# Sample attention's bias rows, spread queries and long bias products, made inside compression

## What is computed

```python
def nsa_global(q, qpos, kv_cmp, kv_slc, p, rel_bias):
    blk, end_pos = compress_blocks(kv_cmp, p["cmp_w"], p["cmp_pe"])      # "compression"
    kc = rmsnorm(blk[:, :, 0], p["nsa_qk_norm"][1])
    o_cmp, p_cmp = cmp_attention(q, qpos, kc, blk[:, :, 1], end_pos, rel_bias)
    idx, valid = select_blocks(p_cmp, qpos, end_pos, n_slc)
    ...                                                                  # selected 64-token blocks
    bias = rel_g[rel_bucket(dist), gi[..., None]]                        # one bias per bucket and head
    pr = masked_softmax(s + bias, mask, axes=(-2, -1))

def sample_layer(...):
    o_cmp, o_slc = nsa_global(q, pos, full_c, full_s, p, rel_bias)
    o_win = win_attention(q[:, None], pos[None, :], win_kv[:, None], kpos, rel_bias)[:, 0]
    o_mem = mem_attention(qm, cache_mem)
    y = layer_tail(x, gb, o_pool, o_nsa, o_mem, p)                       # ends in the experts
```

## Time and profile before

| | |
|---|---|
| median of 3 runs | 1854.88 us (1852.64 to 1856.59) |
| the profiled execution, its own time | 1856.81 us |
| its span, first to last instruction | 1854.8 us |
| mean granted TensorE clock | 0.949 of full speed |
| PE busy | 1714.4 us (92%) |
| DVE, ACT, POOL busy | 550.5, 338.1, 449.9 us |
| compression | from 175 to 303 us |
| sample attention | from 304 to 382 us |

### The profile page before, as it was taken

How to read it: one execution, slowest core, us unless ns; L and a number is a source line. 1 busy time by engine, 2 the same in 40 slices (tenths; PEclk the granted TensorE clock), 3 DMA queues, 4 the chain that set the end, 5 groups by cost and what they waited for, 6 DMA issues and landing times.

```text
span 1854.8 us, 40016 instructions
## 1 busy us (share of the span) xinstructions
PE 1714.4 (92%) x16080; PEld 953.3 (51%) x16080; DVE 550.5 (30%) x1391; ACT 338.1 (18%) x740; POOL 449.9 (24%) x520
## 2 busy tenths in 40 slices
PE   7998997679799999879999999999999999999992
PEld 3446785244478884534465754444444444444441
DVE  1333113446401113453232313231323232323235
ACT  3232112146400001101111111111111111111110
POOL 1122326647400006011212212221212222222220
PEclk9997997779999999879999999999999999999996
DMA  9534757850251103339999999999999999999986
GB/s 342 198 104 150 252 162 221 278 210 2 84 165 57 52 25 119 139 151 404 425 422 425 416 421 411 428 423 421 422 421 408 427 423 420 423 420 406 430 338 248
DMA packets 86641, 541.98 MB, mean 292 GB/s; under 512 B 19888, under 2 KB 44048, under 8 KB 73617
## 3 DMA queue, kind: packets, MB, share of 16 engines
q1 hardware_dynamic: 64809, 498.50, 66.8%
q0 software_dynamic: 14544, 32.03, 5.1%
q10 hardware_dynamic: 7232, 10.73, 1.8%
HBM read 523.39 MB, written 29.78 MB: 298 GB/s over the span
## 4 chain that ended last, share of the span: by engine, by line
PE 54%; DMA 1%; DVE 0%; issue 0%; SPq 0%; POOLq 0%; POOL 0%; ACT 0%
PE psum L2987 36%; PE psum L3013 18%; DMA arena<-y_of 1%; PE psum L2997 0%; DVE arena L2977 0%; SPq L2826 0%; SPq L2828 0%; DMA y_of<-arena 0%; DMA arena<-scr_h,arena 0%; DVE arena L2920 0%; POOL arena L2857 0%; POOLq L2788 0%; ACT arena L2906 0%; POOLq L2861 0%; POOLq L2857 0%
## 5 line engine op out<-in xcount | busy, mean ns | idle before, releaser
L2987 PE MATMUL psum<-arena 128*32 128x512 f32 x6144 | 668.2, 592 | 2.7 <-issue 2.7
L2987 PEld LDWEIGHTS psum<-arena 128*32 128x32 f32 x6144 | 234.4, 108 | 417.0 <-issue 413.3
L3013 PE MATMUL psum<-arena 128*32 128x256 f32 x6144 | 344.9, 378 | 0.0
L3013 PEld LDWEIGHTS psum<-arena 128*32 128x32 f32 x6144 | 236.0, 109 | 110.0 <-issue 9.6
L2942 DVE TENSOR_TENSOR arena<-psum,arena 128x512 f32<-128x512 f32 x96 | 66.5, 692 | 582.4 <-PE psum L2987 582.4
L2874 POOL DMA_INDIRECT y_of<-arena x96 | 97.0, 1011 | 476.2 <-ACT arena L2906 476.2
L2902 ACT ACTIVATE arena<-arena 128x256 f32<-128x256 f32 x96 | 40.1, 418 | 610.1 <-DVE arena L2944 610.1
L2618 PE MATMUL psum<-arena 128*128 128x272 f32 x608 | 144.3, 395 | 1.6 <-PEq L235 1.6
L2618 PEld LDWEIGHTS psum<-arena 128*128 128x128 f32 x608 | 116.1, 191 | 28.5 <-issue 3.3
L2853 POOL DMA_INDIRECT arena<-scr_h,arena x96 | 98.8, 1030 | 48.9 <-POOL arena L2849 28.2
L878 PE MATMUL psum<-arena 128*128 128x512 f32 (+1 forms) x256 | 97.4, 541 | 12.7 <-DMA arena<-in_w_tok 10.1
(11 more groups left out here) (369 smaller groups left out, 1520.5 us busy)
## 6 DMA issues: line engine op xcount, KB each, us to landing
arena<-in_w_gu SPq DMA_DIRECT2D x64, 4096.0 KB, 15.1
arena<-in_w_down SPq DMA_DIRECT2D x32, 4096.0 KB, 14.5
arena<-in_w_gb SPq DMA_DIRECT2D x24, 512.0 KB, 4.5
arena<-y_of SPq DMA_DIRECT2D x8, 1024.0 KB, 15.3
arena<-in_cache_cmp SPq DMA_DIRECT2D x62, 128.0 KB, 3.1
arena<-in_cache_slc SPq DMA_DIRECT2D x60, 128.0 KB, 6.5
arena<-in_x_all SPq DMA_DIRECT2D x8, 512.0 KB, 11.3
arena<-in_w_tok SPq DMA_DIRECT2D x2, 2048.0 KB, 14.0
```

The costliest lines, as they stand in the source:

```text
L2987: mm = pe.matmul(gu_bank(g)[32 * j:32 * j + 32].rearrange("p (h n) -> p h n", h=2), xgT[:, g, 32 * k:32 * k + 32], gu_w(slot)[:, part, :, ...
L3013: mm = pe.matmul(dn_half(g)[32 * j:32 * j + 32], actT[:, g, 32 * k:32 * k + 32], dn_w(slot)[:, part, 256 * j:256 * j + 256], start=(k == 0 ...
```

## The change

The 14 DVE instructions that fill `rel_rows`, `q_rows` and `qm_rows`, with their three clears, move into compression, into a function `tables()` that DVE runs once, after `after(3)` and ahead of the copies of fill product 3. The four long bias products move to the end of PE's compression list: one ahead of `blocks(8)`, two ahead of `keys(8)`, one after it. Sample attention begins with the three short products; PE marks the four banks as full at once. ACT copies the banks in the order 2, 3, 0, 1. `q_rows` and `sc_m` swap places in SBUF, so that `q_rows` doesn't lie in memory that compression uses; the sizes of the two are the same.

```diff
                 for s in range(NS - 1):
                     after(s)
+                    if s == 3:
+                        tables()
                     if s < FILL:
...
+                pe.wait_ge(s_sc, 16 * 12)
+                pe.wait_ge(s_rr, 4)
+                def far_bias(*quarters):
+                    for q in quarters:
+                        pe.matmul(bank(q), rel_rows, oh_slc[:, 512 * q:512 * q + 512], start=True, stop=True).then_inc(s_b3, 1)
+                far_bias(2)
                 blocks(NS)
+                far_bias(3, 0)
                 keys(NS)
+                far_bias(1)
+                pe.wait_ge(s_qr, 12)
...
             def _(act):
-                for b in range(4):
+                for b in (2, 3, 0, 1):
                     filled(act, b, "bias", b)
+                    act.wait_ge(s_b3, 4)
                     copy(bias_slc[:, 512 * b:512 * b + 512], bank(b)).then_inc(free[b], 1)
...
             def _(dve):
-                dve.wait_ge(s_sc, 16 * 12)
-                link(dve.memset(rel_rows, 0.0))
-                for t in range(TS):
...
-                link(dve.memset(q_rows, 0.0))
-                link(dve.memset(qm_rows, 0.0))
...
             def _(pe):
-                pe.wait_ge(s_sc, 16 * 12)
-                pe.wait_ge(s_rr, 4)
+                for q in range(4):
+                    pe.sem_inc(full[q], 1)
                 pe.matmul(bank(5)[:, 0:NCMP_S], rel_rows, oh_cmp, start=True, stop=True).then_inc(full[5], 1)
                 pe.matmul(bank(6)[:, 0:32], rel_rows, oh_new, start=True, stop=True).then_inc(full[6], 1)
                 pe.matmul(bank(4), rel_rows, oh_win, start=True, stop=True).then_inc(full[4], 1)
-                for q in (2, 3, 0, 1):
-                    pe.matmul(bank(q), rel_rows, oh_slc[:, 512 * q:512 * q + 512], start=True, stop=True).then_inc(full[q], 1)
-                pe.wait_ge(s_qr, 12)
```

More of the change, by code:

```diff
@@ L988, in build_program @@
         probT = take(17, 128)
-        q_rows = take(NS, 32)
+        sc_m = take(MEM)
         p_cmp = take(2, 128)
@@ L1009, in build_program @@
         stats = take(2, 24)
-        sc_m = take(MEM)
+        q_rows = take(NS, 32)
         assert cursor[0] <= early_base
@@ L1094, in build_program @@
         s_bh = sem("s_bh")
+        s_rr, s_qr, s_b3 = sem("s_rr"), sem("s_qr"), lasting("s_b3")
         f_p, f_e, f_s = sem("f_p"), sem("f_e"), sem("f_s")
@@ L1247, in after, with tables @@
                     dve.tensor_tensor(kn[0:n], kn[0:n], gain_kc[0:n], ALU.mult).then_inc(s_kn, 1)
+                def tables():
+                    dve.wait_ge(s_sc, 16 * 12)
+                    link(dve.memset(rel_rows, 0.0))
+                    for t in range(TS):
+                        q = slice(32 * t, 32 * t + 32)
+                        dst = rel_rows[q].rearrange("b (s h t) -> b t s h", s=4, t=TS)[:, t]
+                        dve.tensor_copy(dst, rel4[q].unsqueeze(1).to_broadcast([32, 4, 8])).then_inc(s_rr, 1)
+                    link(dve.memset(q_rows, 0.0))
+                    link(dve.memset(qm_rows, 0.0))
+                    for g in range(2):
+                        q = slice(64 * g, 64 * g + 64)
+                        for p in range(4):
+                            dst = q_rows[q].rearrange("d s (p g t) -> d g p s t", p=4, g=2)[:, g, p]
+                            dve.tensor_copy(dst, qT[q, p, NP_TOK:].rearrange("d (s t) -> d s t", t=TS)).then_inc(s_qr, 1)
+                    for mp in range(2):
+                        for m2 in range(2):
+                            q = slice(64 * m2, 64 * m2 + 64)
+                            m = 2 * mp + m2
+                            dve.tensor_copy(qm_rows[q, mp, :, 4 * m:4 * m + 4],
+                                            qmT[q, mp, NP_TOK:].rearrange("d (s t) -> d s t", t=4)).then_inc(s_qr, 1)
                 for s in range(NS - 1):
                     after(s)
+                    if s == 3:
+                        tables()
                     if s < FILL:
@@ L1345, in _ @@
                     products(NS, c)
+                pe.wait_ge(s_sc, 16 * 12)
[4 more added lines that the diff above has]
+                far_bias(2)
                 blocks(NS)
+                far_bias(3, 0)
                 keys(NS)
+                far_bias(1)
+                pe.wait_ge(s_qr, 12)
         phase_over()
-        s_rr = sem("s_rr")
-        s_qr = sem("s_qr")
         s_d3 = sem("s_d3")
```

14 lines of the change are left out of this document (removed).

## The result

The changed kernel takes 1857.75 us (median of 20 runs, 1853.71 to 1861.54) against 1855.02 us for the kernel before (20 runs beside them): a ratio of 1.0016, 95% interval 1.0010 to 1.0022. That is 3.0 us slower (1.9 to 4.1), inside the 0.2% that I called no change, and 2.4 us above the 1855.4 that I predicted. The profiled execution took 1861.06 us, its span 1859.2; it is one of the two longest of the 20.

What follows compares the result with a forecast made beforehand. Two issue queues, SP's and POOL's, starting at the barrier were taken to bound sample attention. Fills 0, seam 0.2, early start 0 and clock 0.3 gave 0.5 us slower, 1855.4 us, range 1851.5 to 1859.2.

Steps and rivals of the forecast that it cites:

- The bound: Sample attention: it runs at the pace of SP's and POOL's issue queues from the barrier; the bias path is hidden.
- The early start arrives: Rival, sample attention: SP's and POOL's lists are paced by PE, so 7.4 us pass into the time, 1847.5; chance 0.10.
- The early start: Start of sample attention: small(0) begins at about 307.0 instead of 314.42, 7.4 us earlier; 0 of it arrives.
- Round 0's last quarter: Score n = 5 in sample attention: it needs the 16th gather, delayed by DVE's addition; gain about 0.9 us.
- The seam: Barrier between compression and sample attention: moved long products cost between 0 and 1.5 us; 0.2 taken.
- the rival of the grown seam: Compression's end: PE outlasts POOL's drain at half clock throughout, 1.5 us, 1856.4; chance 0.10.
- The clock: Sample attention, round 0: PE falls to 1.2 GHz, memory_rows(0) ends later, memory loads leave 0 to 0.4 late; 0.3 taken.
- The slow rival: Sample attention, n = 5 to selected_rows(0): half clock through round 0's end, 4.1 us remain, 1859.2; chance 0.16.
- The sum: Whole kernel: fills 0, seam 0.2, early start 0, clock 0.3, together 0.5 us slower, 1855.4 us.

Runs made afterwards that it cites:

- e5_sem_beside: Changed kernel with its new lasting semaphore s_b3 created beside the lasting s_sc, not among the phase's own: 1854.17 us, 0.9998 to the kernel before.
- e2_products_twice: Changed kernel with the four long products made a second time at their old place, ACT waiting for those: 1858.08 us, 1.0013 to the kernel before.
- e3_no_long_products: Changed kernel without the four long products and without s_b3, so its result isn't the reference's: 1857.2 us, 1.0006 to the kernel before.
- e9: Changed kernel, s_b3 beside s_sc, page loads shared out among SP, ACT and POOL, four of ACT's behind the exponential: 1850.8 us, 0.9977.
- e10: Kernel before with page loads shared out among SP, ACT and POOL, four of ACT's behind the exponential: 1855.47 us, 1.0004.
- e1: Changed kernel with the long products back at their old place and no s_b3; only the fills stay in compression: 1856.73 us, 1.0013 to the kernel before.
- e4_warm_waits: Changed kernel with four unused 512-column products ahead of each of the scores n = 4 and n = 5: 1856.04 us, 1.0003 to the kernel before.
- e11_warm_sem_beside: Changed kernel with s_b3 beside s_sc and four unused products ahead of each of n = 4 and n = 5: 1855.55 us, 0.9999.
- e6_six_holes: Kernel before with six unused lasting semaphores strewn among those of the phase: 1856.5 us, 1.0011.
- e12_neutral_edit: Kernel before with q_rows and sc_m exchanged in SBUF and an unused lasting semaphore beside s_sc, no work moved: 1855.29 us, 0.9999.

## Why the prediction was right, and where it was not

**The bound held.** That the bias path lies in the shadow of two issue queues is shown from three sides: the changed kernel starts 8.1 us earlier and has 0.5 us of it at the memory score, and none in e5_sem_beside's time; e2_products_twice and e3_no_long_products move PE's start by 2.8 and 1.4 us against it with no effect that the times show; and with the queue ahead of the memory loads halved, 6.7 of 7.7 us arrive in the profiles and 5 in the time (e9 against e10). "The early start arrives" was a rival with the right condition: it needed lists that PE paces, and these lists are not.

**The early start was a little larger than my 7.4 us.** `small(0)` came 8.1 us earlier. I had it near 307.0 on the clock of the kernel before, T + 2.2; it was T + 1.45, as the three short products took 1.47 us (306.98 to 308.45) and not the 2.7 that I kept for them: PE now comes to them from the long products, and its granted clock was 1.00 from 303 to 306 us.

**Round 0's last quarter.** I gave n = 5 a gain of 0.9 us, less than 2 because the 2048-column addition on DVE would fall on a gather of round 0. It did: the gather at 320.75 took 2.85 us, beside 2.13 before. I had used the price of before (1.2 us over a plain gather); it was 1.9, as the gather met the addition earlier. So the 16th gather left at T + 20.65 and not at T + 18.76, and n = 5 was about 0.4 us earlier. POOL's whole list is 0.6 us longer for it. The sentence of the Trainium skill that I had set against this row ("SBUF — State Buffer", section Who interferes with whom: an addition of two SBUF operands doesn't stall descriptor making, which the page calls inferred) again disagrees with the measurement, and the measurement decides. I had left out that the same section has such an addition contend with a POOL instruction that reads SBUF; a gather reads `arena` (its operands in the earlier trace rows), so that sentence agrees with the 2.85 us.

**The seam.** Forecast 0.2, measured 0.14 (6.07 to 6.21), of which 0.04 is the split clear, by e5_sem_beside; without the products (e1, e3) it was 6.08. The first product ran at 1.2 GHz (2.02 us for its two passes), and the clock rose during the next two, as I had allowed. PE ended at 304.50, and POOL's drain at 288.0 + 17.1 = 305.1:

```profile
L1104 POOLq DRAIN  x1: 17117/17117/17117, 288.0 to 288.0; - x1
```

So PE stayed within the cover of POOL's drain, and the rival of the grown seam fell.

**The clock: the mechanism was right and the size too small.** I had 0.3 us, from an SP list that holds the loads until 332.05 and a `memory_rows(0)` at 332.4. The pause of SP is 1.30 us in the changed profile. The step that failed is the start of n = 5: with the gather lengthened by 1.9 us rather than 1.2, n = 5 gained 0.4 us and not 0.9, and then lost 0.9 us to the slow clock, as did `memory_rows(0)`. The memory loads left 0.53 us later than before on T's count, as SP's list itself ran 0.7 us shorter. The size isn't a constant either: in e5_sem_beside, with the clock at 0.50 and 0.56 in the same stretches and a gather of 2.34 us, the pause is 0.35 us. e4_warm_waits shows the cause and e11_warm_sem_beside that it is not worth anything one can measure by itself. The slow rival (half clock through to `selected_rows(0)`) came only in part: `turn_selected(0)` took 1.97 us again, and round 0 ended at 342.6, T + 35.6, ahead of the memory data at T + 38.3; it needed 343.65, T + 38.8.

**The term that was missing.** "The sum" had no place for what a phase's end does with a new semaphore. The change's one word `lasting`, in a line with two semaphores of the phase, split the clears: about 0.7 us in the rows of three seams, with e5_sem_beside taking it back and e6_six_holes making longer seams in a kernel without the change. So against the 0.5 us of the forecast the rows hold 1.35: compression's seam 0.14, sample attention's 0.52, the prompt attention's 0.16, and SP's pause with at most the 0.53 by which the memory loads leave later on T's count; e11_warm_sem_beside against e5_sem_beside, and the memory score, which came 0.48 us earlier, speak for nothing of it. Of the 3.0 us measured (1.9 to 4.1), 1.6 or more are left that these rows don't hold. Between the memory score and the seam at its end the changed profile loses 2.0 us on the kernel before (the window's data come later, and the products behind them are slower), but e5_sem_beside's loses nothing there, and e12_neutral_edit, without the change, loses 1.4. I leave that rest open, with the 2.4 us of e1_fills_only. So the forecast was right in its bound and in the early start that doesn't arrive; that the total still came within the range, with a term missing and this rest open, is owed to the width of the range and not to the sum.

## What to carry to other kernels

Before shortening a path, read the DMA issue lists beside it: here a list that starts at a barrier and has no wait in it issued at the same times however early the engines were ready, and the saving arrived only once the list was shorter; done together, the two were worth 4 us here (e9_queues_after_2, 0.9977), while either alone was worth nothing. Put a semaphore that outlives its phase beside others of its kind, since each one strewn among a phase's own made the ends of later phases longer. And where a phase ends on waits for data, compare seams and issue times, and take the verdict from repeated runs: two profiles of the same work differed by 2.6 us in this phase.

## What was not expected of the hardware

- A clear of semaphores with its drain costs about 0.14 us at a phase's end (19 more for 2.6 us at three seams of e6_six_holes), with PE and POOL waiting; one more cost 0.52 us at the end of sample attention in the changed kernel.
- A gather on POOL beside DVE's addition of 128x2048 float32 (2.29 us) took 2.85 us in the changed kernel, 2.13 in the kernel before, against 0.95 alone: the price depends on when in the addition the gather begins (0.26 us behind its start here, 0.98 before). In all 14 profiles each of the two gathers that began during such an addition, 28 in all, ended 3.1 us after the addition's start, some 0.8 us behind its end, and took 1.9 to 3.0 us; a gather already running when an addition began took 0.95 us as elsewhere.
- PE's granted clock fell to 0.50 in the stretch in which it waited 3.25 and 3.82 us with one score of 1.80 us between, and eight unused products in these waits kept it at 1.00.
- The DMA engines moved 357 GB/s at a share of 1.02 to 1.04 for 24 us of the phase, in kernels with quite different issue lists; in the first 24 us the lists held them at 203 GB/s.
